# Norms of a two-layer block computed by token: small sums, roots and reciprocals, the scale spread by TensorE

## The reference

```python
def rmsnorm(x, w):
    y = xf * lax.rsqrt(jnp.mean(xf * xf, axis=-1, keepdims=True) + EPS)
    return (y * w).astype(x.dtype)

hn = rmsnorm(h, norm_mix_w)                     # mix1
proj = hn @ w_in; ...                           # attention and SSD
h = h + concat([att, ssd]) @ w_out
hn = rmsnorm(h, norm_mlp_w)                     # mlp
h = h + square(relu(hn @ w_ff1)) @ w_ff2
x = rmsnorm(h, norm_final_w)                    # end1
h = rmsnorm_2(x, norm_mix_g)                    # mix2
z = h @ w_in; ...                               # gMLP and forgetting attention
x = x + merged @ w_out
h2 = rmsnorm_2(x, norm_ffn_g)                   # ffn2
up = causal_depthwise_conv_2(h2 @ w_up, conv_w, conv_b)
x = x + (gelu(up[..., :D_FF_2]) * up[..., D_FF_2:]) @ w_down
h3 = rmsnorm_2(x, norm_ple_g)                   # ple
x = x + (p @ w_ple) * sigmoid(h3 @ w_ple_gate)
return rmsnorm_2(x, norm_final_g)               # end2
```

## Time and profile before

| | us |
|---|---|
| median of 3 runs | 1744.99 (1744.84 to 1745.13) |
| profiled execution, its own time | 1743.77 |
| its span | 1741.9 |
| TensorE busy | 1663.5 (95%) |
| VectorE busy | 987.7 (57%) |
| ScalarE busy | 666.2 (38%) |
| GpSimd busy | 162.8 (9%) |
| granted TensorE clock, mean | 0.982 |
| weight splits `w_hi` on ScalarE, 131 | 250.2 |
| weight splits `w_lo` on VectorE, 131 | 299.9 |

### The profile page before, as it was taken

One profiled execution on the slowest core, in us unless ns is written; L12 is line 12 of the kernel. 1 busy time (PEld: TensorE's weight loads), 2 busy tenths in 40 slices (PEclk: granted clock), 3 DMA queues, 4 the chain that ended last, 5 costly groups with the idle time before them and its releaser, 6 DMA issues.

```text
span 1741.9 us, 20362 instructions
## 1 busy us (share of the span) xinstructions
PE 1663.5 (95%) x8330; PEld 1387.5 (80%) x8330; DVE 987.7 (57%) x1356; ACT 666.2 (38%) x1007; POOL 162.8 (9%) x236
## 2 busy tenths in 40 slices
PE   6999999999999999999999999999998999999996
PEld 4778888777888888878898887888887788788774
DVE  6654657756434343566754458544556636646757
ACT  4432237544232323432564135541334414414443
POOL 3000003510000000001630036100000000000001
PEclk9999899999999999999999999999999999999998
DMA  4121113122222222233112211322232222222221
GB/s 176 61 76 58 49 40 106 49 73 77 97 97 98 97 95 99 97 115 128 59 58 97 73 73 49 122 97 97 97 109 75 94 97 97 97 97 97 97 97 49
DMA packets 24172, 153.15 MB, mean 88 GB/s; under 512 B 3344, under 2 KB 3728, under 8 KB 6928
## 3 DMA queue, kind: packets, MB, share of 16 engines
q1 hardware_dynamic: 21168, 145.76, 23.4%
q10 hardware_dynamic: 2912, 6.09, 1.0%
HBM read 147.65 MB, written 4.19 MB: 87 GB/s over the span
## 4 chain that ended last, share of the span: by engine, by line
PE 69%; DVE 18%; ACT 7%; issue 4%; POOL 1%; DMA 0%; ACTq 0%; DVEq 0%; SPq 0%; POOLq 0%
PE bank L523 17%; PE bank L525 17%; PE bank L524 17%; DVE w_lo L1368 5%; DVE up_c L1897 4%; PE bank L533 3%; PE bank L535 3%; PE bank L534 3%; ACT w_hi L941 2%; ACT up_c L1300 2%; DVE conv L1574 1%; PE bank L681 1%; PE bank L666 1%; DVE up_g L1902 1%; PE bank L784 1%
## 5 line engine op out<-in xcount | busy, mean ns | idle before, releaser
L523 PE MATMUL bank<-a_hi,w_hi 128*128 128x512 f32 x1216 | 485.4, 399 | 27.5 <-DVE w_lo L1368 14.2
L525 PE MATMUL bank<-a_hi,w_lo 128*128 128x512 f32 x1216 | 477.1, 392 | 0.0
L524 PE MATMUL bank<-a_lo,w_hi 128*128 128x512 f32 x1216 | 477.1, 392 | 0.0
L941 ACT ACTIVATE w_hi<-w_raw 128x2048 fp32r<-128x2048 f32 x131 | 250.2, 1910 | 248.1 <-DMA w_raw<-in_strips 246.4
L1368 DVE TENSOR_TENSOR w_lo<-w_raw,w_hi 128x2048 fp32r<-128x2048 f32 x131 | 299.9, 2289 | 5.9 <-ACT w_hi L941 5.7
L523 PEld LDWEIGHTS bank<-a_hi,w_hi 128*128 128x128 f32 x1216 | 231.1, 190 | 80.0 <-DVE w_lo L1368 17.3
L525 PEld LDWEIGHTS bank<-a_hi,w_lo 128*128 128x128 f32 x1216 | 230.4, 190 | 48.9
L524 PEld LDWEIGHTS bank<-a_lo,w_hi 128*128 128x128 f32 x1216 | 231.0, 190 | 46.8 <-issue 1.0
L523 PE MATMUL bank<-b_hi,w_hi 128*128 128x512 f32 x560 | 218.7, 391 | 3.3 <-DVE w_lo L1368 2.3
L524 PE MATMUL bank<-b_lo,w_hi 128*128 128x512 f32 x560 | 218.0, 389 | 0.0
L525 PE MATMUL bank<-b_hi,w_lo 128*128 128x512 f32 x560 | 217.9, 389 | 0.0
(11 more groups left out here) (302 smaller groups left out, 1958.3 us busy)
## 6 DMA issues: line engine op xcount, KB each, us to landing
w_raw<-in_strips SPq DMA_DIRECT2D x132, 1024.0 KB, 4.8
x<-in_x_t SPq DMA_DIRECT2D x4, 512.0 KB, 8.3
head_bias<-in_rel ACTq DMA_DIRECT2D x1, 2048.0 KB, 11.6
x_kept<-x ACTq DMA_DIRECT2D x1, 2048.0 KB, 6.3
x<-x_kept SPq DMA_DIRECT2D x1, 2048.0 KB, 9.3
out<-out_t SPq DMA_DIRECT2D x8, 256.0 KB, 2.2
w_raw<-in_strips SPq DMA_DIRECT2D x2, 512.0 KB, 5.2
ws_t<-in_ws_t ACTq DMA_DIRECT2D x1, 512.0 KB, 5.4
```

Source lines behind the costliest of these rows:

```text
L523: mm(ps[:, :], w_hi[slot][:, k, cols], hi[:, k, :], start=(k == 0), stop=False)
L524: mm(ps[:, :], w_hi[slot][:, k, cols], lo[:, k, :], start=False, stop=False)
L525: return mm(ps[:, :], w_lo[slot][:, k, cols], hi[:, k, :], start=False, stop=(k == kt - 1))
L941: run(w_hi[j], w_raw[j], ACT.Copy).then_inc(hi_split, 1)
```

## The change

1. **Small norms.** `stat` no longer multiplies `ones` by the sums; it uses each 128x128 block of `sq_sum` as the stationary side and one column of ones as the moving one (`column_sums`), so the sum comes out as [128x4], tokens in the partitions. Scaling, root and reciprocal run on [128x4] (`norm_tok`, or `rstd_tok` for mix1 and mix2).
2. **Spread.** `spread` puts the scale back into all partitions with four products of the column, repeated 128 times, and the identity; VectorE copies the bank to `rstd` (`keep_spread`). It is issued inside the stream, behind k = 2 of fill 2, and in `qk2a` behind the small projection of fill 1. `turn_rstd` and `rstd_by_token` are gone.
3. **Tables.** The first activation of the kernel loads the root's table; `load_sqrt` loads it behind attention 1, behind the last sigmoids of `gate_a` and behind the last `up_group`.
4. **Splits.** In `ff1_0`, `qk2a`, `up0` and `gate` the split pair of the phase's third strip moves from behind the first evacuation to ahead of the norm, on both engines.
5. **Outputs.** In end2 the last three sums are taken apart and added by VectorE; the scale is spread into two banks. VectorE multiplies straight from bank 5, ScalarE copies bank 4 to `rstd` for GpSimd.

```diff
-            def stream(phase, part, act, ready=None, after=None, strips=0, fills=0, kt=KT):
+            def stream(phase, part, act, ready=None, after=None, strips=0, fills=0, kt=KT, within=None):
...
-                            last.then_inc(unit_done, 1)
+                                if k == kt - 1:
+                                    last.then_inc(unit_done, 1)
+                                if within is not None:
+                                    within(j, k)
...
-                mm(where[:, :], ones, total, start=True, stop=True).then_inc(NORMS[norm]["stat"], 1)
-
-            def turn_rstd(norm):
+                column_sums(where, 0, total).then_inc(NORMS[norm]["stat"], 1)
+
+            def column_sums(where, at, total):
+
+                for t in range(TT):
+                    last = mm(where[:, at + t:at + t + 1], total[:, t * P:(t + 1) * P], ones[:, 0:1], start=True, stop=True)
+                return last
+
+            def spread(norm, where=STAT[0], tok=norm_tok):
 
                 n = NORMS[norm]
                 pe.wait_ge(n["rstd"], 1)
                 for t in range(TT):
-                    last = tr(bank[7][:, t * P:(t + 1) * P], rstd[:, t * P:(t + 1) * P], ident)
-                last.then_inc(n["turned"], 1)
+                    last = mm(where[:, t * P:(t + 1) * P], tok[:, t:t + 1].to_broadcast([P, P]), ident, start=True, stop=True)
+                last.then_inc(n["stat"], 1)
...
+            def spread_soon(norm, tok=norm_tok):
+                return lambda j, k: spread(norm, tok=tok) if (j, k) == (2, 2) else None
...
                     stat("mix2", sq_g_sum, STAT[1])
                     small_columns(1, A)
-                if j == 3:
-                    turn_rstd("mix2")
+                    spread("mix2", STAT[1], rstd_tok)
+                    spread("end1", STAT[0])
...
             pe.wait_ge(n["sum"], KT - 2)
-            mm(STAT[1][:, :], ones, sq_sum, start=True, stop=False)
+            column_sums(STAT[1], 0, sq_sum)
             pe.wait_ge(n["sq"], KT - 1)
-            mm(STAT[1][:, :], ones, sq[KT % 2], start=False, stop=False)
+            column_sums(STAT[1], TT, sq[KT % 2])
             pe.wait_ge(n["sq"], KT)
-            mm(STAT[1][:, :], ones, sq[(KT - 1) % 2], start=False, stop=True).then_inc(n["stat"], 1)
+            column_sums(STAT[1], 2 * TT, sq[(KT - 1) % 2]).then_inc(n["stat"], 1)
+
+            spread("end2", STAT[1])
+            spread("end2", STAT[0])
...
+            def load_sqrt():
+
+                run(wait_note[:, 0:1], zeros, ACT.Sqrt)
...
-            run(exp_a[:, 0:1], gains[:, 0, 0:1], ACT.Copy).then_inc(act_evac, 2)
+            run(exp_a[:, 0:1], gains[:, 0, 0:1], ACT.Sqrt, scale=0.0).then_inc(act_evac, 2)
...
-            root("ffn2", rstd)
+            hi(FIRST["up0"] + 2)
+            root("ffn2", norm_tok[:, 0:TT])
...
-                        if fill % 2 == 0:
+                        if fill % 2 == 0 and (g or fill):
                             hi(FIRST[f"up{g}"] + fill // 2 + 2)
...
             up_group(UP_TILES // KT, UP_TILES % KT)
+            load_sqrt()
...
-            root("end2", rstd)
+            root("end2", norm_tok[:, 0:TT])
             last_gain(KT - 1)
+
+            act.wait_ge(NORMS["end2"]["stat"], 3)
+            run(rstd, STAT[0][:, :], ACT.Copy).then_inc(NORMS["end2"]["std"], 1)
...
-            def inverse_rms(norm, e, where=STAT[0], to=rstd):
+            def inverse_rms(norm, e, tok=norm_tok[:, 0:TT]):
                 n = NORMS[norm]
                 dve.wait_ge(n["stat"], 1)
-                v.tensor_scalar(to, where[:, :], 1.0 / D, e, ALU.mult, ALU.add).then_inc(n["var"], 1)
+                v.tensor_scalar(tok, STAT[0][:, 0:TT], 1.0 / D, e, ALU.mult, ALU.add).then_inc(n["var"], 1)
                 dve.wait_ge(n["std"], 1)
-                v.reciprocal(to, to).then_inc(n["rstd"], 1)
-                dve.wait_ge(n["rstd"], 1)
-
-            def rstd_by_token(norm):
+                v.reciprocal(tok, tok).then_inc(n["rstd"], 1)
+                keep_spread(norm)
+
+            def keep_spread(norm, where=STAT[0], to=rstd):
                 n = NORMS[norm]
-                dve.wait_ge(n["turned"], 1)
-                v.tensor_copy(rstd_tok, bank[7][:, :].rearrange("p (t c) -> p t c", t=TT)[:, :, 0]).then_inc(n["tok"], 1)
-                dve.wait_ge(n["tok"], 1)
+                dve.wait_ge(n["stat"], 2)
+                v.tensor_copy(to, where[:, :]).then_inc(n["rstd"], 1)
+                dve.wait_ge(n["rstd"], 2)
...
+            lo(FIRST["up0"] + 2)
             inverse_rms("ffn2", EPS2)
...
-                        if fill % 2:
+                        if fill % 2 and (g or fill > 1):
                             lo(FIRST[f"up{g}"] + fill // 2 + 2)
...
             for m in range(KT - POOL_OUT):
                 dve.wait_ge(x_scaled_out, m + 1)
-                v.tensor_tensor(out_t[m], x[:, m, :], rstd, ALU.mult).then_inc(out_ready, 1)
+                v.tensor_tensor(out_t[m], x[:, m, :], STAT[1][:, :], ALU.mult).then_inc(out_ready, 1)
```

More of the change, by code:

```diff
@@ L499, in _ @@
             pool.wait_ge(x_scaled_out, KT)
-            pool.wait_ge(NORMS["end2"]["rstd"], 1)
+            pool.wait_ge(NORMS["end2"]["std"], 2)
             for m in range(KT - POOL_OUT, KT):
@@ L615, in turn_small @@
             def turn_small(which, norm):
-                pe.wait_ge(NORMS[norm]["tok"], 1)
+                pe.wait_ge(NORMS[norm]["rstd"], 1)
                 pe.wait_ge(small_ready, 8)
@@ L708, in turn_xs @@
                 else:
-                    pe.wait_ge(NORMS["mix1"]["var"], 1)
+                    pe.wait_ge(NORMS["mix1"]["rstd"], 2)
                 src = xs_t[m % 2] if m < 8 else bc_t[:, m - 8, :]
@@ L719, in after_xbc @@
                     stat("mix1", sq_sum, STAT[0])
-                if j == 3:
-                    turn_rstd("mix1")
                 if j >= 3:
                     turn_xs(j - 3)
-            stream("xbc", feature_k, A, ready=wait_tiles(NORMS["mix1"]["lo"]), after=after_xbc)
+            def spread_soon(norm, tok=norm_tok):
+                return lambda j, k: spread(norm, tok=tok) if (j, k) == (2, 2) else None
+            stream("xbc", feature_k, A, ready=wait_tiles(NORMS["mix1"]["lo"]), after=after_xbc,
+                   within=spread_soon("mix1", rstd_tok))
             small_columns(0, A)
@@ L833, in ff_group @@
                 stream("ff1_0", feature_k, A, ready=wait_tiles(NORMS["mlp"]["lo"]), strips=8 * g, fills=16 * g,
-                       after=(lambda j: stat("mlp", sq_sum, STAT[0]) if j == 0 else None) if norm else None)
+                       after=(lambda j: stat("mlp", sq_sum, STAT[0]) if j == 0 else None) if norm else None,
+                       within=spread_soon("mlp") if norm else None)
                 stream("ff2_0", feature_k, B, ready=lambda k: pe.wait_ge(ff_lo, KT * g + k + 1), strips=8 * g, fills=16 * g)
@@ L897, in up_group @@
                 stream("up0", feature_k, A, ready=wait_tiles(NORMS["ffn2"]["lo"]), strips=12 * g, fills=24 * g,
-                       after=(lambda j: stat("ffn2", sq_sum, STAT[0]) if j == 0 else None) if norm else None)
+                       after=(lambda j: stat("ffn2", sq_sum, STAT[0]) if j == 0 else None) if norm else None,
+                       within=spread_soon("ffn2") if norm else None)
                 stream("down0", feature_k, B, ready=lambda k: pe.wait_ge(up_lo, KT * g + k + 1), strips=12 * g, fills=24 * g)
@@ L1054, in _ @@
                 act.dma_start(w16_raw[:, j], d["w16"][j]).then_inc(consts_loaded, 16)
-            root("mix1", rstd)
+            root("mix1", rstd_tok)
             act.wait_ge(consts_loaded, 16 * N_CONST)
@@ L1167, in _ @@
                     hi(FIRST["wo_att"] + 3)
-            root("mlp", rstd)
+            hi(FIRST["ff1_0"] + 2)
+            root("mlp", norm_tok[:, 0:TT])
             def ff_group(g):
@@ L1202, in _ @@
             act.dma_start(shift.rearrange("p g t -> p (g t)"), d["bs"].partition_broadcast(P)).then_inc(late_loaded, 16)
-            root("mix2", rstd, 1.0 / D)
-            root("end1", rstd1)
             hi(FIRST["qk2a"] + 2)
+            root("mix2", rstd_tok, 1.0 / D)
+            root("end1", norm_tok[:, 0:TT])
             keep_small(1)
@@ L1336, in _ @@
                     hi(FIRST["ple"] + 2)
-            root("ple", rstd)
+            hi(FIRST["gate"] + 2)
+            root("ple", norm_tok[:, 0:TT])
             def last_gain(m):
@@ L1552, in _ @@
                             ALU.subtract).then_inc(small_ready, 1)
-            inverse_rms("mix1", EPS1)
+            inverse_rms("mix1", EPS1, rstd_tok)
             v.memset(w16.bitcast(F32), 0.0).then_inc(w16_ready, 1)
@@ L1714, in _ @@
             lo(FIRST["wo_att"] + 3)
+            lo(FIRST["ff1_0"] + 2)
             inverse_rms("mlp", EPS1)
@@ L1927, in _ @@
             lo(FIRST["ple"] + 2)
+            lo(FIRST["gate"] + 2)
             inverse_rms("ple", EPS2)
@@ L1932, in _ @@
```

(4 more changed lines are left out.)

44 lines of the change are left out of this document (24 added, 20 removed).

## The result

In the comparison that followed the forecast the kernel before took 1745.06 us (median of 4 runs, 1744.84 to 1745.63) and the changed kernel 1729.51 (4 runs, 1728.37 to 1731.04): ratio 0.9911, 95% interval 0.9894 to 0.9928. That is 15.5 us less, where 7.95 were forecast; 1729.5 lies under the range. The changed kernel's profiled execution has a span of 1726.6 (1741.9 before).

A forecast was written before the change was run, and what follows sets the result against it. TensorE carries 69% of the chain, but VectorE and ScalarE set up0's pace. Terms -1.8 -0.4 +2.0 -4.9 -2.85 sum to -7.95, from 1744.99 to 1737.0 us; range 1734.5 to 1739.5, with 1733.5 to 1741.9 at 8 to 9 in 10.

The forecast's parts named there:

- mix1: First norm, before xbc: first tap earlier, constants late next; -1.8 us, bounds -1.2 and -2.6.
- mlp, end1 and mix2: In mlp the 1.59 wait in ff1_0 goes, net -0.4; in end1 and mix2 sums and spreads add +2.0.
- ffn2: Norm ahead of up0: first evacuation 0.9 earlier and the split pair leaves round one (-4.0), together -4.9.
- ple: TensorE never waits there, so one sum +0.33 and one spread +0.89 give +1.2 for all behind.
- end2 without ple's lag: Final norm and outputs: earlier scale, faster products, data end near 1738.2 instead of 1741.05; -2.85 with ple's lag included.
- I subtract 7.95 from 1744.99: Whole kernel: the terms' sum of -7.95 taken from the median of three runs gives 1737.0.
- spreads after 9 matmuls: In mix1 TensorE spreads after nine matmuls from 26.12, at 28.2 to 29.1, and VectorE's copy ends at 29.95.
- F: Rival: more gain from mix1's constants being no limit, cheaper sums and the clock staying up in xbc; 1733.5, chance 0.09.
- Rival C: Small products cost double where TensorE is the bound, 0.9 each, +7: 1744, chance 0.05.
- B: Rival: up0 gives its gain back, the third strip's split or GELU's table load ending round one; 1741.9, chance 0.09.
- D: Rival: early split delays VectorE's norm and TensorE stands still, 2.2 at each of five places; 1748, chance 0.03.
- rival E: Table loads pay 1.3 more before end2's root and before p_hi, +2.7 together: 1739.8, chance 0.03.

The follow-up runs named there:

- b_keep: Kernel before with the z-stage copy edit and thrown-away products in TensorE's stalls, without the three ahead of end2's spreads: 1723.56 us, 0.9909.
- s_keep: a_stage with thrown-away products in TensorE's stalls in mix1, turn_small, z, wo_att, attention 2b and end2: 1716.41 us, 0.9884.
- experiment 1: Both kernels rerun unchanged, before 1736.53 and changed 1729.84 us; also with six products repeated ahead of a fill of qk, 1734.21 and 1735.61.
- experiment 2: Both kernels with VectorE copying z's next chunk operands ahead of its split, removing TensorE's stall: before 1728.32, changed 1722.75 us.
- a_stage: Changed kernel with VectorE copying z's next chunk operands ahead of its split: 1722.75 us, 0.9920 to the kernel before.
- b_stage: Kernel before with VectorE copying z's next chunk operands ahead of its split: 1728.32 us, 0.9958 to the unedited kernel.
- experiment 3: a_stage with the memset of w16 moved ahead of mix1's norm on VectorE: 1721.54 us, 0.9916.
- experiment 6: a_stage with VectorE's five output products reading the scale from its SBUF copy in place of the PSUM bank: 1725.45 us, 0.9932.
- Experiment 4: a_stage with five, two and three thrown-away products behind the three sums of end2: 1720.82 us, 0.9922.
- experiment 7: a_stage with thrown-away products in TensorE's stalls (1716.41 us), then also the w16 memset moved and end2's two spreads in the other order (1715.08).
- after: The changed kernel's profile in the first comparison, span 1726.6 us; its four runs have a median of 1729.51.
- s_outsb: a_stage with VectorE's five output products reading the scale from SBUF instead of the PSUM bank: 1725.45 us, 0.9932.
- s_best: s_keep with the w16 memset ahead of mix1's norm and end2's two spreads in the other order: 1715.08 us, 0.9876.
- s_fill: a_stage with thrown-away products behind the three sums of end2, old order of the spreads: 1720.82 us, 0.9922.

## Why the prediction was wrong, point by point

The terms, from the starts of the same instructions in the profiles of `b_keep` and `s_keep` (where the clock hardly plays a part), beside the forecast:

| term | forecast | measured |
|---|---|---|
| mix1 (up to the stall at strip 2) | -1.8 | -0.8 |
| mlp, end1 and mix2 | +1.6 | +0.3 |
| ffn2 | -4.9 | -5.0 |
| ple | +1.2 | +0.9 |
| end2 without ple's lag | -4.05 | -2.4 |
| drift between stages | | -0.3 |
| sum | -7.95 | -7.3 |

**The step that failed** is the first line of the sum: "I subtract 7.95 from 1744.99", as if the kernel before had one time. It has two, 1733 and 1745, and the changed kernel 1728 and 1738. The three runs that were shown agreed within 0.3 us, and the first comparison set, by luck, the upper group of one against the lower of the other: 4.7 between the lower groups, 11.9 from the lower to the upper group of before, less 1.1 by which the changed kernel's four runs lie above the lower group's median, is 15.5. The trace of before did hold a warning that I passed over: in `z` the granted clock is 0.88 over 88 us, with a fall behind each stall of 1.77, while none follows the stall of 1.59 in `ff1_0`. I looked at the clock only in stages that the change touches, and wrote a range from the bounds of its edits alone, with nothing for the clock in the others. What the runs showed in its place: the same stall in `z` costs 9.2 us of clock in one execution and none in the next (experiment 1), and with the stall gone from both kernels 5.57 us are left of the change (experiment 2), less than the 7.95 forecast and not more. The measured 15.5 thus speak neither for nor against the terms of the sum.

**mix1.** -1.8 became 0.0 in the profile after (the stall at strip 2 ends at 46.24, before 46.28) and -0.9 in `a_stage`, where the clock stayed up (45.33 against 46.21 in `b_stage`). The forecast's chain was right (the constants are what is late next, experiment 3: 32.36 against the forecast's 31.7), but "spreads after 9 matmuls" took these at full clock. In the profile after they run at half clock with the sum (the spread starts 5.5 us behind the sum's start, in `a_stage` 3.5), and the copy and the memset come too late. F's hope that the clock would stay up in `xbc` was not met either: it is at 0.50 from 43.9 to 50.8, and before the change from 41.8 to 52.0.

**Sums and spreads.** I took 1.19 for a sum from the products of L622. In the stream it takes 0.81, which is 0.06 less than the old one: halfway between my +0.33 and the lower bound of -0.4. A spread takes 0.81 against 0.89. With three sums and three spreads that makes 1.4 us in mlp, end1 and mix2, where 1.3 were missing, and 0.5 in ple, where it was 0.3. Rival C is out: small products do not cost double.

**mlp and ffn2.** Right, stall and pair by the number: 19.01 between first and fifth evacuation for "about 19", 22.93 for the next round, 3.9 back in round one when the pair goes back; the rest of the 5.0 is the earlier first evacuation, 1.1 for a forecast of 0.9. Nothing became late in its place, so B and D are out.

**end2.** The root right behind the table load, the reductions, the products at 0.61 and GpSimd's 3.70 came as forecast, and experiment 6 shows by its reverse that the PSUM operand is the cause. What failed is the price of the spread (0.89 each, taken from a busy stage): TensorE had stood idle between the sums, ran at half clock and took 1.9 each. Experiment 4 gives 1.7 of the 2.0 us that are missing back. The order of the spreads, where GpSimd gets the second, was no part of it: with the clock up both orders end 13.8 us behind the last `x` addition (experiment 7), and the remaining 0.3 are not explained.

**The drain of rival E** is not there: the root starts 0.02 us behind a load of 1.28, as in the earlier trace rows. By the Trainium skill (ScalarE: Activation LUTs, What ACT_TABLE_LOAD costs) a switch would cost as much again; the measurement decides, and it shows the load alone.

## What to carry to other kernels

Before you forecast from a profile, look for short stalls of TensorE with half clock behind them in every stage, touched or not: behind each the clock may fall in one run and not in the next, and three runs that agree don't show that the kernel has one time. If it has two, take the stall away in both kernels (or keep TensorE at work in it) and compare those; the 12 us between the groups were more than the change itself, and taking the stall away was worth nearly as much as the change. Price TensorE's work behind an idle stretch at half clock, small products above all: that is where norms and tails stand.

## What the runs showed of the hardware

- A stall of 1.77 us is followed by a granted clock of 0.50 for 6.8 us in one execution and by none in the next of the same program; each such fall cost 3.1 us in z. Thrown-away products in a stall mostly keep it up (three profiles of three at `turn_small` and in attention 2b), not always (`s_keep`, 1702.4 to 1705.8).
- Four one-column fp32 products with a 128-column stationary side take 0.81 us from start to start at full clock (mlp, `after`), as much as four of 128 columns, and 1.70 at half (24.94 to 26.64 in mix1, `after`).
- A tensor-tensor product of VectorE with one PSUM operand takes 0.61 from start to start beside GpSimd's products, with two SBUF operands up to 1.75, and GpSimd's three take 3.7 against 5.1 (`a_stage`, `s_outsb`).
- With 377 GB/s the DMAs of the last outputs are at their limit in `s_best` (DMA share 1.03): GpSimd ends 0.9 us earlier there than in `s_fill`, the first store goes out 0.9 later, and the kernel ends as late.
